# Delta stage of a hybrid DeltaNet and attention encoder: the first step of each group is stored and loaded ahead, GpSimd takes some elimination columns, the scaling moves

## The chip, the cores and the metric

The kernel runs on one core of a Trainium2 chip. The metric is the device time of the whole program in microseconds, the lower the better. Three runs of the kernel before took 4063.66, 4072.95 and 4077.66 us; the median is 4072.95 us.

## The reference, cut to what matters

The model has two layers over 2048 tokens of width 1024. In each layer one projection feeds two branches: a bidirectional gated DeltaNet with 4 heads of 128, and a grouped-query attention. Their gated outputs go through one output projection. The change touches the DeltaNet branch only, whose core is this recurrence, run once forward and once on the flipped sequence:

```python
lower = jnp.where(strict, jnp.einsum('bnhid,bnhjd->bnhij', k_beta, kc) * decay, 0.0)
a_mat = lower + jnp.eye(C, dtype=lower.dtype)
sol = lax.linalg.triangular_solve(a_mat, rhs, left_side=True, lower=True, unit_diagonal=True)
u, w = sol[..., :Dv], sol[..., Dv:]
def step(state, inp):
    v_new = u_i - jnp.einsum('bhcd,bhde->bhce', w_i, state)
    o_i = (jnp.einsum('bhcd,bhde->bhce', q_i * jnp.exp(g_i)[..., None], state)
           + jnp.einsum('bhij,bhje->bhie', a_i, v_new))
    state = state * jnp.exp(g_last)[..., None] + jnp.einsum('bhcd,bhce->bhde', k_dec, v_new)
```

So each chunk of tokens needs the inverse of a triangular matrix with ones on its diagonal, and the chunks of a direction follow each other through the state.

## The kernel before, in words

The program is a sequence of stages for each layer: input projection, tables, delta stage (`delta_net`), attention, output projection. The stages are separated by barriers. Inside a stage each engine works through its own list in the written order, and semaphores tie the lists together. All DMAs of the delta stage are issued by SyncE (SP), in the order in which its list is written; SP stands still at a wait, and everything later in its list stands with it.

The delta stage works on 16 chunks of 128 tokens (`NC = 16`), 4 heads, and two sides (forward and backward). It has two phases.

In the local phase TensorE forms the products k k^T and k q^T of every chunk, and VectorE multiplies them with the decays (`products`, L1438 and L1441) into `w` and `att`. SP stores the diagonal blocks of 32 x 32 of each `w` to DRAM (`w_blk`) and loads them back so that each of up to 128 partitions, a lane, holds one block. A block is inverted by elimination of 31 columns (`eliminate`); a column is a multiplication and a subtraction over all lanes. There are four groups of lanes (`GROUP_STEPS`): group 0 holds the blocks of scan steps 0 to 3, group 1 those of steps 4 to 7, and so on. Two sets of lane buffers are used in turn. Group 0 is eliminated on VectorE between the chunks (`LOCAL_COLS`), the others on GpSimd during the scan (`SCAN_COLS`: in scan step j, which group and how many columns). Afterwards `scale_lanes` (VectorE, L1467 and L1469) and `turn_lanes` (ScalarE, L1272) produce the scaled and the turned form, and SP stores both to DRAM (`store_lanes`, L1011 and L1015, four DMAs of 256 KB; the semaphores are `dt_stored` and `dd_stored`).

In the scan step j takes one chunk of each side. Its matrix inverse is put together from the 32 x 32 inverses, one step ahead: `load_dt(i)` and `load_dd(i)` (L1031, four DMAs of 32 KB each) bring the blocks of step i into `dt` and `dd`, which share the buffer `c_sq_acc`. TensorE multiplies `w` with `dt` (`off_diagonal`), VectorE masks it (`masked_blocks`, L1483), and three rounds of `substitute` on TensorE and `update` on VectorE (L1492, L1495) use `dd`. TensorE's order in step j is: `known`, `carried`, `off_diagonal(j+1)`, `solve(j)`, `turn_k(j+1)`, `substitute(j+1, 1)`, `output(j)`, `substitute(j+1, 2)`, `state_step(j)`, `substitute(j+1, 3)`. VectorE's order is: `remainder(j)` (L1476), `masked_blocks(j+1)`, `update(j+1, 1)`, `visit(j)` (L1505), `update(j+1, 2)`, `new_state(j)` (L1510), `update(j+1, 3)`, and in the steps of `SCALED` the scaling at the end. From step 8 on the output of a chunk is also joined, normalized and gated, and steps after 8 carry that work of the step before.

The four lane stores take 4 steps each as their outermost dimension (`i` in `i (h b) (s t)`). In SP's loop they stood first, in the steps of `STORED` (2, 6 and 9), that is one step after the scaling:

```python
for j in range(NC):
    if j in STORED: store_lanes(STORED[j])
    if j + 2 < NC: load_kq(j + 2)
    if j + 2 < NC: load_dt(j + 2)
    ...
    if j + 2 < NC: load_dd(j + 2)
```

Of the kernel before, what the change touches and what calls it, by code (L numbers as in the profile page):

```python
# [854 lines left out]
GROUP_STEPS = [(0, 4), (4, 8), (8, 12), (12, 16)]  # L855
GROUP_READY = [8, 16]
HALF_LANES = P // 2
CHUNK_LANES = DN_HEADS * N_BLK
# [2 lines left out]
FIRST_VISITS = NC // 2  # L861
COLS = BLK - 1
PARTS = 2 * COLS
LOCAL_COLS = {9: 1, 10: 5, 11: 5, 12: 5, 13: 5, 14: 5, 15: 5}
SCAN_COLS = {0: (1, 14), 1: (1, 17), 2: (2, 9), 3: (2, 10), 4: (2, 12), 5: (3, 9), 6: (3, 11), 7: (3, 11)}
SCALED = {1: 1, 5: 2, 8: 3}
STORED = {2: 1, 6: 2, 9: 3}
LANES_IN = {0: 2, 3: 3}

# [47 lines left out]
def delta_net(nc, a, c, l):  # L918
# [1 line left out]
    names = " ".join(f"{n}{side}" for n in per_side.split() for side in SIDES)  # L920
    names += (" kqv_loaded0 kqv_loaded1 kqv_loaded2 beta_loaded logs sums dts gram qk "
              "vt w att vv w_stored0 w_stored1 zeroed kq_loaded0 kq_loaded1 dt_loaded dd_loaded "
              "lane_loaded0 lane_loaded1 inv_set mat_set part turned scaled dt_stored dd_stored part_stored part_loaded z_loaded "
              "norm_loaded joined squared summed mean root inv_mean normed y_stored")
    with ExitStack() as stack, semaphores(nc, names) as s:
        b = Buffers(nc, stack, f"dn{l}")
# [30 lines left out]
        with nc.Block() as block:  # L957

            @block.sync
            def _(sp):  # L960
# [38 lines left out]
                                     a.b_rows[chunk_of(1, first + m), DN_HEADS:ITEMS].rearrange("h (b s) -> (h b) s", s=BLK)) \  # L999
                            .then_inc(s["beta_loaded"], 16)  # L1000

                def store_lanes(g):
                    first, last = GROUP_STEPS[g]
                    lower = slice(0, (last - first) * CHUNK_LANES)
                    upper = slice(HALF_LANES, HALF_LANES + (last - first) * CHUNK_LANES)
                    if g:
                        sp.wait_ge(s["dt_stored"], 32 * g)
                        sp.wait_ge(s["dd_stored"], 32 * g)
                    sp.wait_ge(s["scaled"], 2 * g + 2)
                    for side, src in enumerate((lanes.mat(g)[lower], lanes.mat(g)[upper])):  # L1010
                        sp.dma_start(a.d_blk[1, first:last, side].rearrange("i h b s t -> i (h b) (s t)"), src) \  # L1011
                            .then_inc(s["dt_stored"], 16)
                    sp.wait_ge(s["turned"], g + 1)
                    for side, src in enumerate((lanes.inv(g)[lower], lanes.raw(g)[upper])):
                        sp.dma_start(a.d_blk[0, first:last, side].rearrange("i h b s t -> i (h b) (s t)"), src) \  # L1015
                            .then_inc(s["dd_stored"], 16)

                def load_kq(i):
                    for side in SIDES:
# [3 lines left out]
                        sp.dma_start(kq[:, i % 2, side], a.proj[T_Q:T_K + DN_HEADS, :, at:at + P].rearrange("f p t -> p f t")) \  # L1023
                            .then_inc(s[f"kq_loaded{i % 2}"], 16)

                def load_blocks(tile, kind, i, loaded, stored):
                    group = sum(i >= last for _, last in GROUP_STEPS)
                    sp.wait_ge(stored, 32 * (group + 1))
                    for k in range(N_BLK):
                        at = slice(k * BLK, (k + 1) * BLK)  # L1030
                        sp.dma_start(tile[at].rearrange("p d h t -> p (d h) t")[:, :, at],  # L1031
                                     a.d_blk[kind, i, :, :, k].rearrange("d h s t -> s (d h) t")).then_inc(loaded, 16)

                def load_dt(i):
                    if i:
                        for side in SIDES:
                            sp.wait_ge(s[f"bt{side}"], i)
                    load_blocks(dt, 1, i, s["dt_loaded"], s["dt_stored"])

                def load_dd(i):  # L1040
                    if i:
                        for side in SIDES:
                            sp.wait_ge(s[f"y{side}"], 3 * i)
                    load_blocks(dd, 0, i, s["dd_loaded"], s["dd_stored"])

                def store_part(i):
                    for side in SIDES:
# [37 lines left out]
                        load_kq((n - 12) // 2)  # L1085
                load_lanes(1)
                sp.wait_ge(s["zeroed"], 2)
                store_lanes(0)
                load_dt(0)
                load_dd(0)  # L1090
                load_dt(1)
                load_dd(1)
                for j in range(NC):
                    if j in STORED:
                        store_lanes(STORED[j])
                    if j + 2 < NC:
                        load_kq(j + 2)
                    if j + 2 < NC:
                        load_dt(j + 2)
                    if j > FIRST_VISITS:  # L1100
                        store_y(j - 1)
                    if j in LANES_IN:
                        load_lanes(LANES_IN[j])
                    if j < FIRST_VISITS:
                        store_part(j)
                    else:
                        load_z(j)
                    if FIRST_VISITS <= j + 1 < NC:
                        load_part(j + 1)
                    if j + 2 < NC:  # L1110
                        load_dd(j + 2)
# [144 lines left out]
            def _(act):  # L1256
# [63 lines left out]
                for j in range(NC):  # L1320
                    for side in SIDES:
                        decayed_state(side, j)
                    if j > FIRST_VISITS:
                        root_mean(j - 1)
                    for side in SIDES:
                        carried_output(side, j)
                    for side in SIDES:
                        new_values(side, j)
                    if j + 1 < NC:
                        for side in SIDES:  # L1330
                            keys(side, j + 1)
                    if j in SCALED:
                        turn_lanes(SCALED[j])
                root_mean(NC - 1)

            @block.gpsimd
            def _(pool):
# [7 lines left out]

                def identity(g):
                    if g >= 2:
                        pool.wait_ge(s["dt_stored"], 32 * (g - 1))
                        pool.wait_ge(s["dd_stored"], 32 * (g - 1))
                    nc.gpsimd.memset(lanes.inv(g), 0.0).then_inc(s["inv_set"], 1)  # L1350
                    pool.wait_ge(s["inv_set"], 2 * g + 1)
                    nc.gpsimd.memset(lanes.diagonal(g), 1.0).then_inc(s["inv_set"], 1)
# [45 lines left out]
                for n in range(NC):  # L1398
                    token_logs(n)
                    if n in (3, 4):  # L1400
                        identity(n - 3)
                    if n == 5:
                        for tile in (dt, dd):
                            nc.gpsimd.memset(tile[:], 0.0).then_inc(s["zeroed"], 1)
                        for side in SIDES:
                            nc.gpsimd.memset(state[:, side], 0.0).then_inc(s[f"state{side}"], 1)
                pool.wait_ge(s["att"], NC)
                for side in SIDES:
                    masked_scores(side, 0)
                done = [0] * len(GROUP_STEPS)  # L1410
                for j in range(NC):
                    if j > FIRST_VISITS:
                        for side in SIDES:
# [20 lines left out]
            def _(dve):  # L1434
# [104 lines left out]
                for n in range(NC):  # L1539
                    products(n)  # L1540
                    if n == 9:
                        prepare_lanes(0)
                    if n in LOCAL_COLS:
                        eliminate(0, done, LOCAL_COLS[n])
                        done += LOCAL_COLS[n]
                scale_lanes(0)
                prepare_lanes(1)
                for side in SIDES:
                    masked_blocks(side, 0)
                for k in (1, 2, 3):  # L1550
# [2 lines left out]
                for j in range(NC):  # L1553
                    more = j + 1 < NC
                    if j > FIRST_VISITS:
                        for side in SIDES:
                            mean_squares(side, j - 1)
                    for side in SIDES:
                        remainder(side, j)
                    if j > FIRST_VISITS:  # L1560
                        inverse_root(j - 1)
                    if more:
                        for side in SIDES:
                            masked_blocks(side, j + 1)
                    if j > FIRST_VISITS:
                        for side in SIDES:
                            gate(side, j - 1)
                    if more:
                        for side in SIDES:
                            update(side, j + 1, 1)  # L1570
                    for side in SIDES:
                        visit(side, j)
                    if more:
                        for side in SIDES:
                            update(side, j + 1, 2)
                    for side in SIDES:
                        new_state(side, j)
                    if more:
                        for side in SIDES:
                            update(side, j + 1, 3)  # L1580
                    if j in SCALED:
                        scale_lanes(SCALED[j])
                for side in SIDES:
                    mean_squares(side, NC - 1)
                inverse_root(NC - 1)
# [694 lines left out]
```

## Time and profile before

| | us |
|---|---|
| median of 3 runs | 4072.95 |
| the profiled execution, whole | 4074.22 |
| its span | 4072.4 |
| TensorE (PE) busy | 3745.9 (92%) |
| VectorE (DVE) busy | 2774.2 (68%) |
| ScalarE (ACT) busy | 1877.4 (46%) |
| GpSimd (POOL) busy | 640.8 (16%) |
| delta stage of the first layer | about 680 to 1080 |
| delta stage of the second layer | about 2680 to 3085 |

Times in the rows count from the start of the span. A row of the order in time gives the start, the busy time, the engine, the line of the kernel, the operation, the tile written and the tiles read, shapes and the count; the square bracket at its end is the idle time of the engine just before it and what ended that. In the names `dn_sb_room` is the working buffer of the delta stage, `dn_sb_kq` the keys and queries of a step, and `c_sq_acc` holds `dt` and `dd`. PEclk is TensorE's granted clock as a share of full speed. The DMA share is the mean busy share of 16 DMA engines.

### The profile page before, as it was taken

What the parts mean: (1) busy time and instruction counts of PE and PEld (TensorE: products, weight loads), DVE (VectorE), ACT (ScalarE), POOL (GpSimd) and SP (SyncE); (2) the same over time, 40 slices, a digit from 0 to 9 for tenths busy, and PEclk for the clock granted to TensorE, in tenths of its full rate; (3) what the DMA queues carried; (4) which work ended last, traced back from release to release, by engine and by line L of the source; (5) the groups of instructions that cost most, each with busy time, mean ns of one, the idle gap of its engine ahead of it and who ended that gap; (6) DMA issues with size and microseconds to landing.
All of it is one profiled execution on the core that took longest, in us unless ns stands there. A gap on an engine that the chain in (4) does not pass through costs nothing. (4 is left out here: it accounts for less than half of the span.)

```text
span 4072.4 us, 55417 instructions
## 1 busy us (share of the span) xinstructions
PE 3745.9 (92%) x18982; PEld 2916.2 (72%) x18982; DVE 2774.2 (68%) x3394; ACT 1877.4 (46%) x2560; POOL 640.8 (16%) x637
## 2 busy tenths in 40 slices
PE   7999997699799999999899999976997999999895
PEld 5877785598667676667678777855895767777674
DVE  6674183666699999975266723836577999999743
ACT  4132212255377777772132222133554777777511
POOL 0022101396300000000001211035852000000000
PEclk9999998899899999999999999988998999999997
DMA  3111174546530000005321113654565100000335
GB/s 119 73 68 73 65 247 155 144 121 174 134 118 22 25 22 25 22 22 187 148 99 68 63 73 127 228 161 112 141 166 181 32 25 22 25 22 21 98 142 232
DMA packets 335332, 407.42 MB, mean 100 GB/s; under 512 B 105825, under 2 KB 254945, under 8 KB 314921
## 3 DMA queue, kind: packets, MB, share of 16 engines
q1 hardware_dynamic: 332152, 384.41, 29.6%
q10 hardware_dynamic: 3024, 20.97, 1.2%
q8 instruction: 94, 1.54, 0.2%
q14 instruction: 62, 0.50, 0.0%
HBM read 265.44 MB, written 139.66 MB: 99 GB/s over the span
## 5 line engine op out<-in xcount | busy, mean ns | idle before, releaser
L1829 DVE TENSOR_REDUCE att_sb_part<-att_banks 128x1 f32<-128x512 f32 x992 | 680.2, 686 | 101.5 <-PE att_banks L1714 87.4
L1816 ACT ACTIVATE att_sb_probs<-att_banks 128x1024 f32<-128x1024 f32 x512 | 525.1, 1025 | 312.7 <-PE att_banks L1742 312.5
L1847 DVE TENSOR_TENSOR att_sb_p_lo<-att_sb_probs,att_sb_p_hi 128x1024 fp32r<-128x1024 f32 x512 | 622.6, 1216 | 19.6 <-ACT att_sb_p_hi L1820 19.5
L1820 ACT ACTIVATE att_sb_p_hi<-att_sb_probs 128x1024 fp32r<-128x1024 f32 x512 | 544.1, 1063 | 16.2
L328 PE MATMUL proj_banks<-proj_sb_h_hi,proj_sb_w_hi 128*128 128x512 f32 x1600 | 500.6, 394 | 13.4 <-DVE proj_sb_pad L522 13.4
L328 PE MATMUL proj_banks<-proj_sb_h_lo,proj_sb_w_hi 128*128 128x512 f32 x1600 | 498.7, 393 | 0.0
L328 PE MATMUL proj_banks<-proj_sb_h_hi,proj_sb_w_low 128*128 128x512 f32 x1600 | 497.8, 392 | 0.0
L1742 PE MATMUL att_banks<-att_sb_q,att_sb_k 68*128 68x512 f32 x1024 | 408.7, 399 | 0.0
L1741 PE MATMUL att_banks<-att_sb_q,att_sb_k 128*128 128x512 f32 x1024 | 406.3, 397 | 1.9 <-DVE att_sb_q L1841 1.9
L1759 PE MATMUL att_banks<-att_sb_p_hi,att_sb_v_hi 128*65 128x512 f32 x1024 | 403.1, 394 | 1.4 <-DVE att_sb_p_lo L1847 1.4
L388 POOL TENSOR_TENSOR c_low_squares<-c_sq_acc,proj_sb_high_squares 128x2048 fp32r<-128x2048 f32 x28 | 141.1, 5038 | 1671.3 <-ACT c_sq_acc L449 1671.3
L1759 PE MATMUL att_banks<-att_sb_p_lo,att_sb_v_hi 128*65 128x512 f32 x1024 | 402.8, 393 | 0.0
L1714 PE MATMUL att_banks<-att_sb_k,att_sb_q 128*128 128x512 f32 x992 | 398.9, 403 | 3.0 <-DVE att_sb_part L1829 2.8
L1759 PE MATMUL att_banks<-att_sb_p_hi,att_sb_v_lo 128*65 128x512 f32 x1024 | 400.8, 391 | 0.0
L328 PEld LDWEIGHTS proj_banks<-proj_sb_h_hi,proj_sb_w_hi 128*128 128x128 f32 x1600 | 301.5, 189 | 88.4 <-issue 14.7
L328 PEld LDWEIGHTS proj_banks<-proj_sb_h_lo,proj_sb_w_hi 128*128 128x128 f32 x1600 | 301.0, 188 | 75.5
L328 PEld LDWEIGHTS proj_banks<-proj_sb_h_hi,proj_sb_w_low 128*128 128x128 f32 x1600 | 301.0, 188 | 72.2
L1119 PE MATMUL dn_banks<-dn_sb_room 128*128 128x128 f32 x2048 | 263.6, 283 | 37.1 <-DMA dn_sb_room<-proj 20.2
L1119 PEld LDWEIGHTS dn_banks<-dn_sb_room 128*128 128x128 f32 x2048 | 249.3, 197 | 58.3 <-DMA dn_sb_room<-proj 25.9
L595 DVE SCALAR_TENSOR_TENSOR proj_sb_out<-proj_sb_pad,proj_sb_taps,proj_sb_out 128x2048 f32<-128x2048 f32 x96 | 276.7, 2882 | 3.4
L522 DVE TENSOR_TENSOR proj_sb_out<-proj_banks,proj_sb_scale 128x1024 f32<-128x1024 f32 x56 | 68.5, 1223 | 272.5 <-PE proj_banks L328 272.5
L1714 PEld LDWEIGHTS att_banks<-att_sb_k,att_sb_q 128*128 128x128 f32 x992 | 189.5, 191 | 79.0 <-DVE att_sb_part L1829 7.0
(229 smaller groups left out, 5337.3 us busy)
## 6 DMA issues: line engine op xcount, KB each, us to landing
proj<-proj_sb_out SPq DMA_DIRECT2D x40, 1024.0 KB, 3.8
dn_sb_kq<-proj SPq DMA_DIRECT2D x64, 512.0 KB, 5.0
proj_sb_w_raw<-in_w_in SPq DMA_DIRECT2D x52, 536.0 KB, 3.6
dn_sb_room<-proj SPq DMA_DIRECT2D x32, 768.0 KB, 4.9
att_sb_q<-att_q SPq DMA_DIRECT2D x64, 256.0 KB, 2.6
x_res<-ahead_delta SPq DMA_DIRECT2D x16, 1024.0 KB, 4.1
proj_sb_pad<-proj SPq DMA_DIRECT2D x24, 512.0 KB, 4.4
proj<-proj_sb_out ACTq DMA_DIRECT2D x12, 1024.0 KB, 4.4
```

Of the source, the lines that this page charges most:

```text
L328: mm = nc.tensor.matmul(ps[:, 2 * half + n, :], w[:, u, k, :], h[:, k, at:at + QB], start=(k == 0 and w is w_hi and h is h_hi), stop=(k == ...
L388: nc.gpsimd.tensor_tensor(low, raw, high[:].bitcast(F32), ALU.subtract).then_inc(s["squares_split"], 1)
L595: nc.vector.scalar_tensor_tensor(out=out[:, u, :], in0=src, scalar=taps[:, u, j:j + 1], in1=out[:, u, :], op0=ALU.mult, op1=ALU.add).then_ ...
L1119: mm = nc.tensor.matmul(out[:, h, :], left[:, h, :], right[:, h, :], start=True, stop=True)
L1714: nc.tensor.matmul(ps[:, 4 + u % 2, :], q1[:, slot, tile * P:(tile + 1) * P], k1[:, slot % 2, keys * QB:(keys + 1) * QB], start=True, stop ...
L1741: nc.tensor.matmul(out, k1[:, slot % 2, keys], q1[:, slot, :], start=True, stop=False)
L1742: mm = nc.tensor.matmul(out, k2[:, slot % 2, keys], q2[:, slot, :], start=False, stop=True)
L1759: mm = nc.tensor.matmul(ps[0:DH + 1, 6 + kv, :], part_v[:, kv, tile, 0:DH + 1], part_p[:, at, m, :], start=opens, stop=(tile == NC - 1 and ...
L1816: nc.scalar.activation(probs[:, pair % 2], ps[:, 2 * (pair % 2):2 * (pair % 2) + 2, :], ACT.Exp, scale=SCALE).then_inc(s["exp_done"], 1)
L1820: nc.scalar.activation(p_hi[:, pair % SLOTS], probs[:, pair % 2], ACT.Copy).then_inc(s["hi_done"], 1)
L1829: nc.vector.tensor_reduce(part[:, w // NQ, w % NQ:w % NQ + 1], ps[:, 4 + w % 2, :], AX.X, ALU.max) \
L1847: nc.vector.tensor_tensor(p_lo[:, pair % SLOTS], probs[:, pair % 2], p_hi[:, pair % SLOTS].bitcast(F32), ALU.subtract).then_inc(s["lo_done ...
```

## The change

Four things change, all in `delta_net`.

1. Group 0's elimination: in the chunks 11 to 15 of the local phase GpSimd takes one column (`BESIDE_COLS`) while VectorE does the products, and VectorE takes 4 instead of 5. The results are chained through the semaphore `part` as before.
2. Group 1: VectorE does its first 6 columns (`AHEAD_COLS`) right after it prepared the lanes, before the scan. GpSimd's share in the steps 0 and 1 falls from 14 and 17 to 12 and 13.
3. `store_lanes` is cut in two: `store_first` stores the first step of a group (four DMAs of 64 KB), `store_rest` the other three steps (four DMAs of 192 KB), with semaphores of their own. `load_dt` and `load_dd` wait for the one or the other, by the step they load. Before the scan the order on SP is now first, `load_dt(0)`, `load_dd(0)`, rest, `load_dt(1)`, `load_dd(1)`. In SP's loop the stores moved from the beginning of steps 2, 6, 9 to the middle of steps 2, 5, 8.
4. `scale_lanes` stands in the middle of a step, between `update(j+1, 1)` and `visit(j)`, in steps 2, 5, 8 (before: at the end of steps 1, 5, 8). `turn_lanes` on ScalarE stands ahead of `keys`.

```diff
-LOCAL_COLS = {9: 1, 10: 5, 11: 5, 12: 5, 13: 5, 14: 5, 15: 5}
-SCAN_COLS = {0: (1, 14), 1: (1, 17), 2: (2, 9), 3: (2, 10), 4: (2, 12), 5: (3, 9), 6: (3, 11), 7: (3, 11)}
-SCALED = {1: 1, 5: 2, 8: 3}
-STORED = {2: 1, 6: 2, 9: 3}
+LOCAL_COLS = {9: 1, 10: 5, 11: 4, 12: 4, 13: 4, 14: 4, 15: 4}
+BESIDE_COLS = {11: 1, 12: 1, 13: 1, 14: 1, 15: 1}
+AHEAD_COLS = 6
+SCAN_COLS = {0: (1, 12), 1: (1, 13), 2: (2, 9), 3: (2, 10), 4: (2, 12), 5: (3, 9), 6: (3, 11), 7: (3, 11)}
+SCALED = {2: 1, 5: 2, 8: 3}
...
+                def store_steps(g, lo, hi, dt_sem, dd_sem):
+                    lower = slice((lo - GROUP_STEPS[g][0]) * CHUNK_LANES, (hi - GROUP_STEPS[g][0]) * CHUNK_LANES)
+                    upper = slice(HALF_LANES + lower.start, HALF_LANES + lower.stop)
+                    for side, src in enumerate((lanes.mat(g)[lower], lanes.mat(g)[upper])):
+                        sp.dma_start(a.d_blk[1, lo:hi, side].rearrange("i h b s t -> i (h b) (s t)"), src).then_inc(dt_sem, 16)
+                    sp.wait_ge(s["turned"], g + 1)
+                    for side, src in enumerate((lanes.inv(g)[lower], lanes.raw(g)[upper])):
+                        sp.dma_start(a.d_blk[0, lo:hi, side].rearrange("i h b s t -> i (h b) (s t)"), src).then_inc(dd_sem, 16)
+                def store_first(g):
+                    if g:
+                        sp.wait_ge(s["dt_first"], 32 * g)
+                        sp.wait_ge(s["dd_first"], 32 * g)
+                    sp.wait_ge(s["scaled"], 2 * g + 2)
+                    store_steps(g, GROUP_STEPS[g][0], GROUP_STEPS[g][0] + 1, s["dt_first"], s["dd_first"])
...
-                    sp.wait_ge(stored, 32 * (group + 1))
+                    sp.wait_ge(first if i == GROUP_STEPS[group][0] else rest, 32 * (group + 1))
...
-                store_lanes(0)
+                store_first(0)
                 load_dt(0)
                 load_dd(0)
+                store_rest(0)
                 load_dt(1)
                 load_dd(1)
                 for j in range(NC):
-                    if j in STORED:
-                        store_lanes(STORED[j])
                     if j + 2 < NC:
                         load_kq(j + 2)
+                    soon = j in SCALED and GROUP_STEPS[SCALED[j]][0] == j + 2
+                    if soon:
+                        store_first(SCALED[j])
                     if j + 2 < NC:
                         load_dt(j + 2)
+                    if j in SCALED:
+                        if not soon:
+                            store_first(SCALED[j])
+                        store_rest(SCALED[j])
...
+                col = 0
+                for n in LOCAL_COLS:
+                    if n in BESIDE_COLS:
+                        eliminate(0, col, BESIDE_COLS[n])
+                        col += BESIDE_COLS[n]
+                    col += LOCAL_COLS[n]
                 pool.wait_ge(s["att"], NC)
...
                 scale_lanes(0)
                 prepare_lanes(1)
+                eliminate(1, 0, AHEAD_COLS)
...
+                    if j in SCALED:
+                        scale_lanes(SCALED[j])
                     for side in SIDES:
                         visit(side, j)
```

GpSimd's `identity` waits for all four store semaphores of the group that used the buffers before.

## Rows read from the trace of the kernel before

**Rows 1.** The waits of the delta stage, first layer; columns: who, for whom, us in total, times, longest.

```profile
PE dn_banks L1119 <- DMA c_sq_acc<-d_blk: 38.0, 5, 29.4
```

**Rows 2.** TensorE in order of time, start of the scan and a plain step, first layer.

```profile
792.48 3.75 PE L1119 MATMUL dn_banks<-c_sq_acc,dn_sb_w 128*128 128x128 f32 x16 [29.44 <-DMA c_sq_acc<-d_blk]
...
801.49 3.84 PE L1119 MATMUL dn_banks<-dn_sb_state,dn_sb_kq 128*128 128x128 f32 x32
...
816.67 3.84 PE L1119 MATMUL dn_banks<-dn_sb_state,dn_sb_kq 128*128 128x128 f32 x32
...
820.35 1.95 PE L1119 MATMUL dn_banks<-c_sq_acc,dn_sb_w 128*128 128x128 f32 x16
...
824.79 1.95 PE L1119 MATMUL dn_banks<-c_sq_acc,dn_sb_room 128*128 128x128 f32 x16
...
831.86 3.84 PE L1119 MATMUL dn_banks<-dn_sb_state,dn_sb_kq 128*128 128x128 f32 x32
```

**Rows 3.** TensorE in order of time, later step starts and one wait, first layer.

```profile
873.00 3.84 PE L1119 MATMUL dn_banks<-dn_sb_state,dn_sb_kq 128*128 128x128 f32 x32
...
903.38 3.84 PE L1119 MATMUL dn_banks<-dn_sb_state,dn_sb_kq 128*128 128x128 f32 x32
...
918.81 3.84 PE L1119 MATMUL dn_banks<-dn_sb_state,dn_sb_kq 128*128 128x128 f32 x32
...
926.63 3.78 PE L1119 MATMUL dn_banks<-c_sq_acc,dn_sb_w 128*128 128x128 f32 x16 [3.97 <-DMA c_sq_acc<-d_blk]
...
940.59 3.84 PE L1119 MATMUL dn_banks<-dn_sb_state,dn_sb_kq 128*128 128x128 f32 x32
...
993.57 3.84 PE L1119 MATMUL dn_banks<-dn_sb_state,dn_sb_kq 128*128 128x128 f32 x32
...
1009.63 3.84 PE L1119 MATMUL dn_banks<-dn_sb_state,dn_sb_kq 128*128 128x128 f32 x32
```

**Rows 4.** TensorE in order of time, start and step 11 of the scan, second layer.

```profile
2792.79 3.75 PE L1119 MATMUL dn_banks<-c_sq_acc,dn_sb_w 128*128 128x128 f32 x16 [29.04 <-DMA c_sq_acc<-d_blk]
...
2997.77 3.84 PE L1119 MATMUL dn_banks<-dn_sb_state,dn_sb_kq 128*128 128x128 f32 x32
```

**Rows 5.** VectorE in order of time: products, a column, the scaling of groups 0 and 1.

```profile
757.04 0.68 DVE L1438 TENSOR_TENSOR dn_sb_w<-dn_banks,dn_sb_room 128x512 f32<-128x512 f32 x1
...
758.24 0.41 DVE L1453 TENSOR_TENSOR dn_sb_lane_tmp<-dn_sb_lane_mat,dn_sb_lane_inv 128x255 f32<-128x255 f32 x1
...
773.47 1.87 DVE L1467 TENSOR_TENSOR dn_sb_lane_mat<-dn_sb_lane_inv,dn_sb_lane_beta 64x1024 f32<-64x1024 f32 x1
...
835.67 2.90 DVE L1467 TENSOR_TENSOR dn_sb_lane_mat<-dn_sb_lane_inv,dn_sb_lane_beta 64x1024 f32<-64x1024 f32 x1 [3.03 <-POOL dn_sb_lane_inv L1364]
```

**Rows 6.** SP's DMA issues in order of time, first layer.

```profile
776.67 1.20 SPq L1011 DMA_DIRECT2D d_blk<-dn_sb_lane_mat  x2
...
780.32 1.23 SPq L1015 DMA_DIRECT2D d_blk<-dn_sb_lane_raw  x1
...
786.66 17.08 SPq L1031 DMA_DIRECT2D c_sq_acc<-d_blk  x16
...
832.71 1.80 SPq L1031 DMA_DIRECT2D c_sq_acc<-d_blk  x4
```

**Rows 7.** Windows: stretch, length, busy us of the engines, PEclk, DMA share, GB/s.

```profile
784.00:786.00 2.00, 0.00 (x0) 0.00 (x0) 0.00 (x0) 0.00 (x0) 1.69 (x5) 0.50 0.25 104
```

**Rows 8.** DMA issues by tile: count, KB each, median us to landing; 840 to 857, then 680 to 1060.

```profile
dn_sb_kq<-proj SPq DMA_DIRECT2D x2, 512.0 KB, 8.9
...
dn_sb_lane_raw<-w_blk SPq DMA_DIRECT2D x16, 64.0 KB, 2.9
```

**Rows 9.** GpSimd in order of time, first instruction of a column.

```profile
818.00 0.66 POOL L1362 TENSOR_TENSOR dn_sb_lane_tmp<-dn_sb_lane_mat,dn_sb_lane_inv 128x255 f32<-128x255 f32 x1
```

**Rows 10.** VectorE in order of time, inside plain step 1: visit and new state.

```profile
827.67 0.69 DVE L1505 TENSOR_TENSOR dn_sb_room<-dn_banks,dn_sb_room 128x512 f32<-128x512 f32 x1 [0.20 <-PE dn_banks L1119]
...
830.55 0.69 DVE L1510 TENSOR_TENSOR dn_sb_state<-dn_sb_room,dn_banks 128x512 f32<-128x512 f32 x1 [0.51 <-PE dn_banks L1119]
```

More of the change, by code:

```diff
@@ L922, in delta_net @@
               "vt w att vv w_stored0 w_stored1 zeroed kq_loaded0 kq_loaded1 dt_loaded dd_loaded "
-              "lane_loaded0 lane_loaded1 inv_set mat_set part turned scaled dt_stored dd_stored part_stored part_loaded z_loaded "
+              "lane_loaded0 lane_loaded1 inv_set mat_set part turned scaled dt_first dd_first dt_stored dd_stored part_stored part_loaded z_loaded "
               "norm_loaded joined squared summed mean root inv_mean normed y_stored")
@@ L1000, in load_beta, with store_rest @@
                             .then_inc(s["beta_loaded"], 16)
[L1002 to L1005, printed above, removed]
+                def store_steps(g, lo, hi, dt_sem, dd_sem):
[12 more added lines that the diff above has]
+                    store_steps(g, GROUP_STEPS[g][0], GROUP_STEPS[g][0] + 1, s["dt_first"], s["dd_first"])
+                def store_rest(g):
                     if g:
@@ L1008, in store_lanes @@
                         sp.wait_ge(s["dd_stored"], 32 * g)
[L1009 to L1016, printed above, removed]
+                    store_steps(g, GROUP_STEPS[g][0] + 1, GROUP_STEPS[g][1], s["dt_stored"], s["dd_stored"])
                 def load_kq(i):
@@ L1024, in load_kq, with load_blocks @@
                             .then_inc(s[f"kq_loaded{i % 2}"], 16)
-                def load_blocks(tile, kind, i, loaded, stored):
+                def load_blocks(tile, kind, i, loaded, first, rest):
                     group = sum(i >= last for _, last in GROUP_STEPS)
-                    sp.wait_ge(stored, 32 * (group + 1))
+                    sp.wait_ge(first if i == GROUP_STEPS[group][0] else rest, 32 * (group + 1))
                     for k in range(N_BLK):
@@ L1037, in load_dt @@
                             sp.wait_ge(s[f"bt{side}"], i)
-                    load_blocks(dt, 1, i, s["dt_loaded"], s["dt_stored"])
+                    load_blocks(dt, 1, i, s["dt_loaded"], s["dt_first"], s["dt_stored"])
                 def load_dd(i):
@@ L1043, in load_dd @@
                             sp.wait_ge(s[f"y{side}"], 3 * i)
-                    load_blocks(dd, 0, i, s["dd_loaded"], s["dd_stored"])
+                    load_blocks(dd, 0, i, s["dd_loaded"], s["dd_first"], s["dd_stored"])
                 def store_part(i):
@@ L1328, in _ @@
                         new_values(side, j)
+                    if j in SCALED:
+                        turn_lanes(SCALED[j])
                     if j + 1 < NC:
@@ L1331, in _ @@
                             keys(side, j + 1)
-                    if j in SCALED:
-                        turn_lanes(SCALED[j])
                 root_mean(NC - 1)
@@ L1347, in identity @@
                     if g >= 2:
-                        pool.wait_ge(s["dt_stored"], 32 * (g - 1))
-                        pool.wait_ge(s["dd_stored"], 32 * (g - 1))
+                        for stored in ("dt_first", "dd_first", "dt_stored", "dd_stored"):
+                            pool.wait_ge(s[stored], 32 * (g - 1))
                     nc.gpsimd.memset(lanes.inv(g), 0.0).then_inc(s["inv_set"], 1)
@@ L1409, in _ @@
                     masked_scores(side, 0)
-                done = [0] * len(GROUP_STEPS)
+                done = [0, AHEAD_COLS, 0, 0]
                 for j in range(NC):
@@ L1542, in _ @@
                         prepare_lanes(0)
+                    if n in BESIDE_COLS:
+                        done += BESIDE_COLS[n]
                     if n in LOCAL_COLS:
@@ L1570, in _ @@
                             update(side, j + 1, 1)
+                    if j in SCALED:
+                        scale_lanes(SCALED[j])
                     for side in SIDES:
@@ L1580, in _ @@
                             update(side, j + 1, 3)
-                    if j in SCALED:
-                        scale_lanes(SCALED[j])
                 for side in SIDES:
```

## The prediction, made before the kernel ran

> **What bounds the kernel now.** I began with the page: TensorE is busy 92% of the span, so only its idle stretches can be won, and the change touches only the delta stage, which runs once in each of the two layers. The waits of that stage come next. There the matmuls stand 38.0 us on transfers into the block tiles (`c_sq_acc<-d_blk`, which are `dt` and `dd`), 29.4 us of it in one piece [rows 1]. The order in time shows the places. TensorE is idle 29.44 us before the scan (792.48), and its first matmuls then run slowly: step 0 begins 9.01 us later, at 801.49. A plain step takes 816.67 to 831.86 = 15.19 us; in it the off-diagonal product, which needs `dt` of the next step, starts 3.7 us in, and the first substitution, which needs `dd` of the next step, 8.1 us in [rows 2]. A late step with output normalization takes 1009.63 - 993.57 = 16.06 us [rows 3].
>
> Everything above that is a stretch. From step 0 (801.49) to step 11 (993.57) are 192.08 us; nine plain steps and two late ones would be 9 x 15.19 + 2 x 16.06 = 168.83, so layer 1 loses 23.25 us [rows 2, 3]. In the second layer, from the first matmul (2792.79) to step 11 (2997.77) are 204.98 us; less 9.01 and 168.83 this leaves 27.14 us [rows 4]. Layer 1 loses them so: steps 2 and 3, 873.00 - 831.86 - 30.38 = 10.76 us; steps 6 to 10, 993.57 - 903.38 - 3 x 15.19 - 2 x 16.06 = 12.5 us [rows 2, 3]. The first comes from the scaling of group 1: VectorE waits 3.03 us for GpSimd's columns, then scales at 2.90 us an instruction where 1.87 us was the time alone [rows 5]. Step 7 shows a late `dt`: TensorE waits 3.97 us, the next 16 matmuls take 3.78 us instead of 1.95, and the step is 940.59 - 918.81 - 15.19 = 6.6 us longer [rows 2, 3]. So a wait of about 4 us costs 2.6 us more through the lower clock.
>
> **How the group stores leave.** This decides the sum. The four stores of a group (1 MB) are issued from 776.67 to 781.55. The load of `dt` may start when the first two have landed, at 786.66, 10.0 us after their issue, and TensorE gets `dt` at 792.48, 15.8 us after the first issue [rows 2, 6]. In that time the DMA share is 0.25 at 104 GB/s: 4 engines of 16, 26 GB/s each [rows 7]. The stores' outermost dimension is the 4 steps of a group. A transfer that uses all engines waits behind them: the `kq` load next in SP's order takes 8.9 us to land, though it moves data at once on the idle engines [rows 8].
>
> **1. Five columns of group 0 on GpSimd.** On VectorE the two products of a chunk take 758.24 - 757.04 = 1.20 us; a column there is two instructions of 0.41 us with gaps, about 0.9 us for the longest and 0.65 for short ones. GpSimd needs two of 0.66 us and gaps, 1.5 us for the longest [rows 5, 9]. The products read PSUM, and in the rows they keep their 0.68 us. So the GpSimd column is hidden but for 0.3 us: 0.6 to 0.7 us won five times, 3.2 us. Bounds: 0 to 4.3. It counts in full, since VectorE has no gap between the chunks. The first store goes out at 773.45 instead of 776.67.
>
> **2. First step stored apart (group 0).** Each of these stores has 16 rows of 4 KB. The nearest row is the lane load of the same shape: 64 KB land in 2.9 us [rows 8]. SP issues four small DMAs in 1.8 us (832.71), which I take for the four stores and for each set of four loads [rows 6]. `dt` stores out at 773.45 and 773.9, landed 776.8; `load_dt(0)` 776.8 to 778.6, landed 781.0. TensorE starts 11.5 us earlier (11 to 13), step 0 at 790.0.
> Then `load_dd(0)` to 780.4, and the rest of the group (768 KB) goes out. Its outermost dimension is 3 steps, so by the same pattern 3 engines with 256 KB each, exactly the bytes per engine of before. `load_dt(1)` stands behind it and lands 15.8 us later, at 796.2; step 0 wants it at 790.0 + 3.7 = 793.7. Wait 2.5 us and clock: 5.1 us (0 to 6) given back.
>
> **3. Six columns of group 1 on VectorE, its scaling in the middle of step 2.** The six columns (about 3.5 us) lie in VectorE's idle time before the first block product: nothing. GpSimd has fewer columns left (25 instead of 31) and no longer makes VectorE wait. The scaling now stands before `visit`, 10.8 us into the step. Alone it takes 3.2 us (from 773.47 to the first store at 776.67 [rows 5, 6]); beside GpSimd's columns, by 2.90 against 1.87, up to 5. I take 4.2, the middle, since at the 2.90 GpSimd worked on masked scores, longer instructions than columns. Before the new state VectorE has 0.20 and 0.51 us of idle time [rows 10], and 0.6 us lie between the state and the next product. So a step with scaling grows by 4.2 - 1.3 = 2.9 us (1.9 in step 8, where GpSimd has no columns) and is 18.1 us long. Bounds: 1.9 to 3.7. ACT's turn falls where it waits for the state product: nothing.
>
> **4. What SP now holds back.** In loop j SP issues `load_kq`, `load_dt`, then the stores, and only then `store_part` and `load_dd(j+2)`. Before, the stores came one loop later, when the scaling was already done. Now SP waits at them for the scaling of the same step; `dd` of step j+2 stands behind them in SP's order and then behind the rest's 256 KB on three engines. Substitution 1 of step j+1 needs it.
> Group 1 (j = 2, times from the start of step 2): scaled 15.0; first stores landed 18.35; `load_dt(4)` to 20.15, landed 22.6, wanted at 18.1 + 3.7 = 21.8: 0.8 late. The rest goes out at 20.15; a load behind it lands 15.8 later, and the 512 KB of `store_part` at 16 x 26 GB/s add 1.3: `dd(4)` at 37.25. From the substitution to the next step are 7.1 us, plus 2.6 for the clock: step 4 at 46.95. Plain would be 30.38: 16.6 us lost, where 10.76 was.
> Group 2 (j = 5): scaled 15.0, rest out 16.8, `dd(7)` at 16.8 + 15.8 + 1.3 = 33.9, wanted at 18.1 + 8.1 = 26.2. Step 7 at 33.9 + 9.7 = 43.6: 13.2 lost.
> Group 3 (j = 8): scaled 14.0, rest out 15.8, z and part loads add 2.5: `dd(10)` at 34.1. Step 10 at 43.8 against 31.25: 12.55 lost.
>
> **The sum.** Lost in the scan after the change: 5.1 + 16.6 + 13.2 + 12.55 = 47.45 us. Layer 1: 47.45 - 23.25 - 11.5 = +12.7. Layer 2: 47.45 - 27.14 - 11.5 = +8.8. Together +21.5 on the profiled execution's 4074.2 us, which stands 1.3 us above the median of the three runs: 4094 us.
>
> **The rivals.**
> A, the forecast: the rest stores keep 3 engines busy and hold `dd`. 4094 (4080 to 4110), chance 0.57.
> B, faster: a store of 3 steps is spread over all 16 engines (it has 48 rows). It then drains within its issue time of 4.9 us; step 0 doesn't wait, `dd(4)` lands 30.4 after step 2's start (9.7 lost with the clock), `dd(7)` and `dd(10)` are 0.7 and 0.8 late (3.6 and 2.7 lost with the scaling). 16.0 - 23.25 - 11.5 and 16.0 - 27.14 - 11.5: -41.4, 4032 us. Against it: the 4-step store has 64 rows and used 4 engines [rows 7]. It decides from about 10 engines on, where 768 KB drain in 3 us. Chance 0.20.
> C, the rest drains at 26 GB/s per engine from its first byte: 256 / 26 = 9.8 us, and a load behind lands 11.8 after, not 15.8. Step 0 has no wait, the three others lose 4 less: 17.1 less per layer, 4060 us; halfway it is 4077. 
>
> The Trainium skill, "DMA: Bandwidth & Descriptors", section "Why a DMA increments its semaphore by 16 and not by 1", has a rule on this: the number of engines is the largest, up to 16, that divides the slowest dimension not of size 1 on both sides. The share of 0.25 agrees for the whole group. For the new shapes it gives 3 and 16; no row of before shows them. By it B and D would fall and A would stand.
>
> **Chances.** No change is what lies within 0.3% (12 us), about what this kernel's runs can tell. Faster: B, and 0.05 of C: 0.25. The same: 0.09 of C and 0.11 of A: 0.20. Slower: the rest of A, D, 0.02 of C: 0.55. The range 4030 to 4112 takes in B's time and leaves out D and the tails; the likeliest case alone would be 4080 to 4110.
>
> **What would show it.** Right: the first block product near 781 us, after less than 20 us of idle time instead of 29.4; then TensorE waits of 8 to 11 us on `c_sq_acc<-d_blk` at the first substitution of steps 3, 6 and 9, in both layers; a DMA share near 0.19 for 10 us after each rest; the scaling at 4 us or less and followed by `visit`; no wait of VectorE for GpSimd before it. Wrong: waits on `dd` under 3 us, or a share near 1 after the rest stores (B); a first matmul later than 785 us (D).

## The result, and the profile after

The changed kernel takes 4125.1 us (median of 4 runs, 4119.3 to 4125.7) against 4074.9 us before (4 runs, 4063.7 to 4077.7): a ratio of 1.0129, 95% interval 1.0115 to 1.0144. It is slower by 50 us, where 4094 was forecast and 4112 was the upper end. The profiled execution took 4125.4 us with a span of 4123.6, 51.2 us longer than before.

The waits of the first delta stage in the changed kernel, to be read beside [rows 1] of before:

```profile
PE dn_banks L1134 <- DMA c_sq_acc<-d_blk: 46.9, 5, 17.2
```

TensorE in order of time there (start, us, operation, idle time before and its releaser), against [rows 2, 3]: the first block product, the starts of the steps (the rows that read `dn_sb_state`: steps 0 to 5, 7, 8, 10 and 11) and the waits on `dt` (rows with `dn_sb_w`) and `dd` (rows with `dn_sb_room`) between them.

```profile
776.54 3.75 PE L1134 MATMUL dn_banks<-c_sq_acc,dn_sb_w 128*128 128x128 f32 x16 [17.23 <-DMA c_sq_acc<-d_blk]
785.15 3.84 PE L1134 MATMUL dn_banks<-dn_sb_state,dn_sb_kq 128*128 128x128 f32 x32
792.86 3.78 PE L1134 MATMUL dn_banks<-c_sq_acc,dn_sb_w 128*128 128x128 f32 x16 [3.88 <-DMA c_sq_acc<-d_blk]
807.28 3.84 PE L1134 MATMUL dn_banks<-dn_sb_state,dn_sb_kq 128*128 128x128 f32 x32
822.46 3.84 PE L1134 MATMUL dn_banks<-dn_sb_state,dn_sb_kq 128*128 128x128 f32 x32
839.63 5.47 PE L1134 MATMUL dn_banks<-dn_sb_state,dn_sb_kq 128*128 128x128 f32 x32 [0.28 <-DVE dn_sb_state L1531]
858.83 3.79 PE L1134 MATMUL dn_banks<-c_sq_acc,dn_sb_room 128*128 128x128 f32 x16 [9.28 <-DMA c_sq_acc<-d_blk]
868.26 3.84 PE L1134 MATMUL dn_banks<-dn_sb_state,dn_sb_kq 128*128 128x128 f32 x32
...
883.45 3.84 PE L1134 MATMUL dn_banks<-dn_sb_state,dn_sb_kq 128*128 128x128 f32 x32
...
916.48 3.78 PE L1134 MATMUL dn_banks<-c_sq_acc,dn_sb_room 128*128 128x128 f32 x16 [7.80 <-DMA c_sq_acc<-d_blk]
926.09 3.84 PE L1134 MATMUL dn_banks<-dn_sb_state,dn_sb_kq 128*128 128x128 f32 x32
941.28 3.84 PE L1134 MATMUL dn_banks<-dn_sb_state,dn_sb_kq 128*128 128x128 f32 x32
...
975.90 3.79 PE L1134 MATMUL dn_banks<-c_sq_acc,dn_sb_room 128*128 128x128 f32 x16 [8.70 <-DMA c_sq_acc<-d_blk]
984.85 3.84 PE L1134 MATMUL dn_banks<-dn_sb_state,dn_sb_kq 128*128 128x128 f32 x32
1000.91 3.84 PE L1134 MATMUL dn_banks<-dn_sb_state,dn_sb_kq 128*128 128x128 f32 x32
```

The reader sees the forecast picture: TensorE starts after 17 us of idle time instead of 29, and then waits 7.8 to 9.3 us for `dd` at the first substitution of steps 3, 6 and 9. Step 11 begins at 1000.91, 7.3 us later than before [rows 3]. The second layer's first block product and step 11, against [rows 4]:

```profile
2790.18 3.75 PE L1134 MATMUL dn_banks<-c_sq_acc,dn_sb_w 128*128 128x128 f32 x16 [17.25 <-DMA c_sq_acc<-d_blk]
...
3014.80 3.84 PE L1134 MATMUL dn_banks<-dn_sb_state,dn_sb_kq 128*128 128x128 f32 x32
```

There the changed kernel is 3014.80 - 2997.77 = 17.0 us behind, with nearly all of both delta stages done. At the end of the span it is 51.2 us behind, so 34.2 us are lost later, where the diff changes nothing. The waits of the second attention stage (3130 to 3830 us) in the changed kernel:

```profile
ACT att_sb_probs L1840 <- PE att_banks L1766: 159.6, 223, 3.7
DVE att_sb_part L1853 <- PE att_banks L1738: 45.4, 121, 1.4
DVE att_sb_part L1853 <- issue: 27.1, 5, 5.7
...
PEld att_banks L1738 <- DVE att_sb_part L1853: 22.6, 7, 4.3
ACT att_sb_probs L1840 <- DVE att_sb_p_lo L1871: 22.3, 5, 4.7
PE att_banks L1738 <- DVE att_sb_part L1853: 18.9, 7, 3.9
```

The same view of the kernel before (3113 to 3813 us):

```profile
ACT att_sb_probs L1816 <- PE att_banks L1742: 155.5, 236, 2.6
DVE att_sb_part L1829 <- PE att_banks L1714: 40.7, 125, 1.4
...
PEld att_banks L1714 <- DVE att_sb_part L1829: 1.9, 2, 1.1
```

"issue" says that VectorE waited for nothing that the profile shows, 27.1 us in five pieces; the kernel before has no such row in this window. (Both kernels have one other wait with "issue", of 6.1 to 7.1 us, ahead of the loop, at the start of each attention stage.) Two of them in VectorE's order of time, 95.7 us apart, which is one pass of its loop over the attention blocks; a loop of six passes has five back branches:

```profile
3315.91 0.69 DVE L1853 TENSOR_REDUCE att_sb_part<-att_banks 128x1 f32<-128x512 f32 x1 [5.31 <-issue]
...
3411.62 0.69 DVE L1853 TENSOR_REDUCE att_sb_part<-att_banks 128x1 f32<-128x512 f32 x1 [5.71 <-issue]
```

The DMA view of that stage (queue, packets, MB, share) counts the transfers of instructions: 32 in the changed kernel,

```profile
q14 instruction: 32, 0.26, 0.1%
```

and 8 before:

```profile
q14 instruction: 8, 0.07, 0.0%
```

So the suspicion is that VectorE fetches its loop anew at each back branch, the jump from the end of the loop to its start. In the compiled program of the kernel before, VectorE's second attention loop begins at instruction 2856 and its back branch is instruction 3115, 259 further on; the change adds 4 VectorE instructions per layer, so it begins at 2864. The same loop in the first layer, moved by 4 places, shows no such wait in either kernel.

### The profile page after: what moved, and what is told of

Same layout as the page of the kernel before. It is cut to its first block and busy times, and to the rows that moved or that the text cites. A ratio compares the mean times of both kernels' runs of the same rounds, so it can differ in the third digit from the quotient of the medians.

```text
span 4123.6 us, 55463 instructions
## 1 busy us (share of the span) xinstructions
PE 3764.3 (91%) x18982; PEld 2929.8 (71%) x18982; DVE 2767.2 (67%) x3398; ACT 1877.4 (46%) x2560; POOL 638.7 (15%) x633
```

## The experiments

Each one was timed beside the kernel before on its own chip; a ratio is to those runs. Medians of different chips differ by a few us for the same kernel (4070.2 to 4074.9 for the kernel before), so gains between two chips are given relative to their own runs of before. The theories are P (placement of VectorE's loop, against D, something that the delta stage leaves behind) and Q with O (SP is held up by stores on three engines, and by its order, against S, the scaling).

**b_pad8.** The kernel before, its loop moved to where the change put it.

```diff
                 done = 0
+                for n in range(8 if l == 1 else 0):
+                    nc.vector.memset(pad[:, n:n + 1], 0.0)
                 for n in range(NC):
                     products(n)
```

> The kernel before, with eight one-element memsets on VectorE at the start of the second layer's delta stage (nothing reads them; about 0.06 us each, under 0.5 us in all). They put VectorE's second attention loop 8 instructions later in its program, at the very place where the changed kernel has it (instruction 2864 instead of 2856). Theory P (placement: the changed kernel's 34 us in the second attention stage are VectorE fetching its loop anew at each of 5 back branches): the kernel before now shows the same five stalls of L1853 with no releaser, 27 us in all, about 30 instruction packets on q14 in that stage, and 4074 + 34 = about 4108 us. Rival D (the 34 us come from what the delta stage leaves behind: another order of transfers, another state of the queues or of the clock): 4074 us, no such stalls.

4106.1 us, ratio 1.0082 (1.0065 to 1.0099). Eight instructions that do nothing cost 33 to 36 us, and the stall is there, 28.1 us where the changed kernel has 27.1:

```profile
DVE att_sb_part L1832 <- issue: 28.1, 5, 5.8
```

with 31 instruction packets. No part of the change is in this kernel, so D is out and the place alone brings the stall. What it costs shows in the length of the second attention stage, from the memset that opens it to the first `out_sb_w_lo` behind it: 740.9 us in the kernel before, 774.7 in the changed one and 778.2 here. Over all traces it is 774.7 to 778.2 us in the four kernels whose loop begins at 2864 (the changed one, b_pad8, a_spread, a_dd_first) and 740.8 to 744.9 in the nine others, whatever their delta stage does: P is shown.

**a_pad8** and **a_pad64.** The same lines with 8 and 64 in the changed kernel.

> The changed kernel with the same eight memsets: the second attention loop stands at instruction 2872 of VectorE's program instead of 2864. Theory P: if only a loop that begins at the very end of a stretch of instructions is fetched anew, the stalls go: 4125 - 34 = about 4091 us, with the delta stage's losses unchanged. If the bad places reach further than 8 instructions, it stays at 4125. Rival D: 4125 us.

> The changed kernel with 64 such memsets (about 4 us of VectorE at the start of the second layer's delta stage, where it waits for its first load anyway, so at most some us): the loop stands at instruction 2928. Theory P: no stalls, 4091 us (up to 4095 with the memsets). Rival D: 4125 us or a few more.

4095.3 us, ratio 1.0055 (1.0038 to 1.0072), and 4090.2 us, ratio 1.0049 (1.0032 to 1.0066). The row of this loop with "issue" is gone from both, and the second attention stage of a_pad8, 743.4 us long, has:

```profile
q14 instruction: 7, 0.06, 0.0%
```

So the change proper costs 20 to 25 us; 21.5 was forecast.

**b_pad4** and **b_pad12.** The edges, one run each.

> How wide the bad place is: the kernel before with four memsets, loop at instruction 2860. At 2856 it ran without stalls, at 2864 with five. If the bad stretch is only the few places where a loop of 260 instructions reaches into a third block of 256: no stalls, about 4074 us; if it begins between 2857 and 2860: 4108 us.

> The other edge: twelve memsets, loop at instruction 2868 (2872 ran without stalls). If the bad stretch is as narrow as the loop's excess over 256 instructions (some four places): no stalls, about 4074 us; else 4108 us.

4067.8 and 4069.0 us, each with 7 instruction packets in the stage and no such wait; with one run each it is the traces that decide. If the bad places lie together, they lie between 2861 and 2867. The Trainium skill, "Runtime: NRT & Kernel Launch", section "Instruction fetch mechanics", says that most engines hold two blocks of 256 instructions and that a branch to a target outside them waits for a fetch. A loop of 259 or 260 instructions needs a third block only from two or three of 256 places, which agrees with at most seven bad ones here. That the blocks are the cause is argued from the Trainium skill, and where the blocks begin is not known here; the runs show the stall, its place and its price.

**a_spread.** The changed kernel with one store per step.

```diff
-    sp.dma_start(a.d_blk[1, lo:hi, side].rearrange("i h b s t -> i (h b) (s t)"), src).then_inc(dt_sem, 16)
+    for i in range(lo, hi):
+        at = slice((i - lo) * CHUNK_LANES, (i - lo + 1) * CHUNK_LANES)
+        sp.dma_start(a.d_blk[1, i, side].rearrange("h b s t -> (h b) (s t)"), src[at]).then_inc(dt_sem, 16)
```

The stores of `d_blk[0]` go the same way, and the waits for the rest count 96 instead of 32 per group.

> The changed kernel, only that each store of lanes over several steps is one transfer per step (16 partitions of 4 KB each) instead of one over three steps: 12 transfers instead of 4 for a group's rest, whose packets then lie on all 16 DMA engines instead of 3. Order on SP and all else as in the changed kernel, VectorE's program too, so the 34 us in attention stay. Theory Q (the waits of 9.3, 7.8 and 8.7 us on dd per layer are SP held up by the rest stores on three engines): SP issues the four dd loads in about 2 us instead of 6.65 and they land in 3, so 6 to 7 us go at each of six places, and some of step 0's 3.8: 4125 - 40 = about 4085 us. Rival S (the waits come from scaling in the middle of the step, which makes y late, or from SP's order alone): within 5 us of 4125.

4071.1 us, ratio 1.0002 (0.9992 to 1.0011). The changed kernel is 50.2 us above its own runs of before, this one 0.9: 49 us gained (52 by the ratios), where 40 was expected. A window beside the rest store of group 1 (stretch, length, busy us of PE, PEld, DVE, ACT and POOL, PEclk, DMA share, GB/s) in the changed kernel,

```profile
844.00:846.00 2.00, 2.00 (x20) 2.00 (x20) 0.48 (x2) 1.76 (x7) 1.76 (x4) 1.00 0.17 43
```

and with spread stores:

```profile
838.00:840.00 2.00, 2.00 (x20) 2.00 (x20) 0.62 (x1) 1.76 (x7) 1.84 (x4) 1.00 0.84 152
```

A share of 0.17 is about 3 engines of 16 (3/16 is 0.19, and the window before, 842 to 844, has 0.19); spread it is 0.84. SP then issues the four loads of `dd` in 2.00 us instead of 6.65; the changed kernel's SP rows (start, us, operation, count):

```profile
841.18 1.45 SPq L1009 DMA_DIRECT2D d_blk<-dn_sb_lane_mat  x2
842.67 2.10 SPq L1012 DMA_DIRECT2D d_blk<-dn_sb_lane_inv  x1
844.81 1.09 SPq L1012 DMA_DIRECT2D d_blk<-dn_sb_lane_raw  x1
845.95 1.02 SPq L1058 DMA_DIRECT2D dn_part<-dn_sb_room  x2
847.09 6.65 SPq L1040 DMA_DIRECT2D c_sq_acc<-d_blk  x4
```

and with spread stores:

```profile
836.16 2.71 SPq L1011 DMA_DIRECT2D d_blk<-dn_sb_lane_mat  x6
838.92 1.34 SPq L1016 DMA_DIRECT2D d_blk<-dn_sb_lane_inv  x3
840.31 1.35 SPq L1016 DMA_DIRECT2D d_blk<-dn_sb_lane_raw  x3
841.70 0.90 SPq L1065 DMA_DIRECT2D dn_part<-dn_sb_room  x2
842.70 2.00 SPq L1047 DMA_DIRECT2D c_sq_acc<-d_blk  x4
```

TensorE's wait for `dd(4)` falls from 9.28 to 3.43 us:

```profile
846.32 3.78 PE L1141 MATMUL dn_banks<-c_sq_acc,dn_sb_room 128*128 128x128 f32 x16 [3.43 <-DMA c_sq_acc<-d_blk]
```

The scaling stood where it was, so S is out for these waits. Six waits on `dd` of 0.2 to 4.2 us are left, 15 us in both layers together; they belong to SP's order, as the next experiment and a_both_pad8 show.

**a_dd_first.** The changed kernel, only SP's order.

```diff
                         if not soon:
                             store_first(SCALED[j])
-                        store_rest(SCALED[j])
...
                     if j + 2 < NC:
                         load_dd(j + 2)
+                    if j in SCALED:
+                        store_rest(SCALED[j])
```

> The changed kernel with one call moved on SP: store_rest of a group stands at the end of step j, behind load_dd(j + 2), instead of behind load_dt(j + 2); the rest stores keep their three engines, VectorE's program is the same, so the 34 us in attention stay. Theory O (SP's order is the cause): dd comes in time and the six waits of 8 to 11 us on it, 53 us in all, go; but the rest store now starts some 15 us later and drains over three engines, so load_dt of the group's second step, which waits for it, comes late and gives about half back: about 4100 us. Theory E (the three engines are the cause, whichever order): the late dt costs as much as the late dd did, 4120 to 4130 us.

4088.7 us, ratio 1.0031 (1.0018 to 1.0043). It stands 13.8 us above its own runs of before, so against the changed kernel the order alone is worth 36 us (40 by the ratios). The six waits on `dd`, 53.4 us in all, are gone, and `dt` of the group's second step is late instead, by 1.9 to 5.2 us each time, 20.3 us in all:

```profile
864.49 3.61 PE L1135 MATMUL dn_banks<-c_sq_acc,dn_sb_w 128*128 128x128 f32 x16 [5.05 <-DMA c_sq_acc<-d_blk]
```

O holds, with less given back than expected (4100); E, by which the order would not matter, is out. The gains of spread stores and of the order are not to be added: each takes away part of the same waits.

**a_both_pad8.** Spread stores, this order, and the loop moved.

> All three together: the changed kernel with one store per step (all 16 engines), store_rest behind load_dd, and the eight memsets that move VectorE's loop. The one with the spread stores alone ran 4071 us; less 34 us for the loop; less its six remaining waits on dd (3.4, 0.2, 4.2, 2.5, 1.6 and 3.3 us, 15 in all): about 4022 us, if the late rest store does not make dt late. If it does: 4037 us or more.

4014.1 us (4005.4 to 4022.1), ratio 0.9864 (0.9842 to 0.9887): 61 us below the kernel before by the medians, and the fastest of all; 4022 was expected. After its start TensorE waits for no transfer into the block tiles in the first scan; the group's only row is the one before the first block product:

```profile
PE dn_banks L1143 <- DMA c_sq_acc<-d_blk: 16.1, 1, 16.1
```

**b_spread.** The kernel before with its four-step stores split in the same way.

> The kernel before, only that each store of a group's lanes is one transfer per step (16 transfers of 16 partitions instead of 4 over four steps), on all 16 engines instead of four. VectorE's program is unchanged. Of the 23 and 27 us that its two scans lose against plain steps, the waits behind the stores go in part; the wait for the first block product (29 us, stores and loads in a row) gets some us shorter too: about 4045 us. Rival: before's loads wait for scaling and for the order on SP and not for the draining: 4070 us.

4048.7 us, ratio 0.9936 (0.9914 to 0.9957), near the expected 4045: 26 us gained. The change on top of spread stores is then worth another 35 us (4014.1), if SP's order and the loop's place are put right.

**b_cols_pad16.** The kernel before with the columns of the change alone.

```diff
-LOCAL_COLS = {9: 1, 10: 5, 11: 5, 12: 5, 13: 5, 14: 5, 15: 5}
-SCAN_COLS = {0: (1, 14), 1: (1, 17), 2: (2, 9), ...
+LOCAL_COLS = {9: 1, 10: 5, 11: 4, 12: 4, 13: 4, 14: 4, 15: 4}
+BESIDE_COLS = {11: 1, 12: 1, 13: 1, 14: 1, 15: 1}
+AHEAD_COLS = 6
+SCAN_COLS = {0: (1, 12), 1: (1, 13), 2: (2, 9), ...
```

> The kernel before with only the columns changed as in the change: one of each of group 0's last five blocks of columns on GpSimd beside the products, six columns of group 1 ahead of the scan on VectorE; stores, loads and scaling as before. Sixteen unused memsets keep VectorE's second attention loop (at instruction 2878) off the place where it stalled. Step 1 of the prediction: 3.2 us a layer, 4074 - 6 = about 4067 us. Rival: VectorE waits for GpSimd's column as long as its own took: 4074 us.

4060.8 us, ratio 0.9975 (0.9964 to 0.9985): 14 us by the medians, not 6. Group 0 is faster by about what was expected: from the products of chunk 10 to the scaling VectorE needs 30.09 us (738.76 to 768.85), where it needed 32.88 (740.59 to 773.47). The rest comes from the scan, which the expectation had left out: with 25 columns instead of 31 GpSimd is done sooner, and the first scaling (at 827.71) no longer waits for it, where it waited 3.03 us [rows 5]. From the first block product to step 11 it takes 197.93 us instead of 201.09, and in the second layer 199.39 instead of 204.98.

**a_both_whole.** The fastest kernel with group 0 stored whole before its first loads.

```diff
                 store_first(0)
+                store_rest(0)
                 load_dt(0)
                 load_dd(0)
-                store_rest(0)
```

> The fastest one so far (spread stores, store_rest behind load_dd, loop moved), only that in group 0 store_rest stands ahead of load_dt(0) and load_dd(0): the first step is no longer ahead of the rest. It tells what the early first step is worth once the stores leave on all engines. Twelve more stores stand before load_dt(0) on SP, about 0.4 us each. If the first block product comes as late as with the kernel before and spread stores (24 us of idle time instead of 16): 8 us in each layer, 4014 + 16 = about 4030 us. Rival: with spread stores the order does not matter: 4014 to 4018.

4026.0 us, ratio 0.9882 (0.9864 to 0.9899), where 4030 was expected. Against a_both_pad8 that is 12 us more by the medians but 7 by the ratios, whose intervals overlap, so the times alone do not settle it; the traces do. The wait before the first block product is 22.15 us instead of 16.10, in the second layer 21.91 instead of 16.07:

```profile
784.52 3.73 PE L1143 MATMUL dn_banks<-c_sq_acc,dn_sb_w 128*128 128x128 f32 x16 [22.15 <-DMA c_sq_acc<-d_blk]
```

So the early first step is worth 6 us a layer once the stores leave on all engines; with whole groups on four engines before and the rest on three after, it was worth 10.

## Why the prediction was right and wrong

**1. Five columns on GpSimd, 3.2 us.** Right: 2.8 us, borne out by b_cols_pad16. From the products of chunk 10 to the scaling the changed kernel takes 767.70 - 737.61 = 30.09 us, before it was 32.88. VectorE waits 0.18 to 0.32 us for GpSimd's column.

**2. First step stored apart, 11.5 us with the columns.** Right, a little short: from the scaling to the first block product are 776.54 - 767.70 = 8.84 us, before 19.01 [rows 2, 5], so 10.2 us, and 13.0 with the columns. The forecast moment 781.0 came at 776.54, but 3.0 us of this were there when the products of chunk 10 began (737.61 against 740.59), ahead of the first column moved to GpSimd, and are not the change's. The `dt` wait in step 0 was 3.9 us, not 2.5, and the step lost 807.28 - 785.15 - 15.19 = 6.9 us, not 5.1. The 15.8 us that a load waits behind the stores came out as forecast: the rest goes out at 777.04 and TensorE gets `dt` of step 1 at 792.86.

```profile
777.04 1.61 SPq L1009 DMA_DIRECT2D d_blk<-dn_sb_lane_mat  x2
```

**3. Columns ahead and scaling in the middle.** Right in kind, too dear in size. The scaling beside GpSimd takes 3.6 us where 4.2 was taken:

```profile
833.18 2.18 DVE L1488 TENSOR_TENSOR dn_sb_lane_mat<-dn_sb_lane_inv,dn_sb_lane_beta 64x1024 f32<-64x1024 f32 x1
835.40 1.37 DVE L1490 TENSOR_TENSOR dn_sb_lane_mat<-dn_sb_lane_inv,dn_sb_lane_beta 64x1024 f32<-64x1024 f32 x1
836.80 1.29 DVE L1526 TENSOR_TENSOR dn_sb_room<-dn_banks,dn_sb_room 128x512 f32<-128x512 f32 x2
```

Step 2 took 839.63 - 822.46 = 17.2 us, 2.0 more than a plain step, not 2.9; the two other scaling steps 1.6 to 1.8. At the scaling VectorE no longer waits for GpSimd.

**4. What SP holds back.** Right in mechanism and size: the six waits on `dd` are 7.8 to 10.9 us, where 8 to 11 was named as the sign. Lost in steps 2 and 3: 868.26 - 822.46 - 30.38 = 15.4 us (forecast 16.6); steps 5 and 6: 926.09 - 883.45 - 30.38 = 12.3 (13.2); steps 8 and 9: 984.85 - 941.28 - 31.25 = 12.3 (12.55). With step 0 that is 46.9 us in the first scan, against 47.45. That the total is off by only half a microsecond is luck: the terms are off by +1.8, -1.2, -0.9 and -0.2. The experiments bear the cause out from both sides: the engines (a_spread, 49 us) and the order (a_dd_first, 36 us).

**The sum of the delta stages.** +21.5 was forecast, +17.0 stands at step 11 of the second layer, and 20 to 25 us by the runs with the loop out of the bad place. So the central figure of 4094 was about right for the change proper. Rivals B, C and D did not occur: the share beside the rest stores was 0.17 to 0.19 and not near 1 (B), the load behind the rest landed after 15.8 us and not 11.8 (C), and the first block product came at 776.54, not after 785 (D).

**The step that failed** is the first sentence of the reading: "the change touches only the delta stage". It does in the source, not in the program. The sum had no term for what follows, where the same instructions stood 8 places later; it put that stage at nothing, and 34 us were lost there (stage length 774.7 us instead of 740.9). With the 17.0 of the delta stages these are the 51.2 us. Nothing in the rows of before shows this price: 8 instruction packets and no row with "issue" in the loop. What could have been seen is the exposure: behind the edited code stands a VectorE loop whose back branch is 259 instructions on. The Trainium skill, "Runtime: NRT & Kernel Launch", section "Instruction fetch mechanics", warns of branches out of the two blocks that an engine holds. A rival of this kind, with 5 back branches and an unknown price each, was missing, and so the range ended 13 us short.

## What to carry to other kernels

After a change, compare the traces at a landmark behind each stage, the unchanged ones too: here 17 us of the 51 were at the edit and 34 in a stage that the diff doesn't touch. Where an engine runs a loop, an edit ahead of it moves it: look for waits with "issue" once per pass and for more packets on the instruction queue, and settle it by padding the old kernel by as many instructions. Here a store whose outermost dimension was 4 steps kept the DMA share at 0.25 and one of 3 steps at 0.17 to 0.19, while stores of one step reached 0.84, and the few-engine stores held the issuing queue behind them. Splitting them by step gave 26 us to the old kernel and about 50 to the new one, and moving them behind the loads with a near due time gave 36.

## What the runs showed of the hardware

A back branch of VectorE's loop cost 5.2 to 5.8 us of its time from one placement (the loop beginning at 2864, in four kernels) and nothing that shows from six others (beginning at 2856, 2860, 2868, 2872, 2878 and 2928); with what waits for VectorE it was 34.2 / 5 = 6.8 us each. The changed kernel moved 24 more instruction packets in that stage than the kernel before, about 5 for each of these branches. The transfers of instructions during such a stall, in the DMA view of 3309 to 3317 us:

```profile
q14 instruction: 4, 0.03, 1.7%
```

Four packets of 8 KB took part in a stall of 5.31 us while the DMA share was 0.07 (3310.0 to 3315.5), so it is no matter of bandwidth. SP's issue of four block loads, 1.80 us in the kernel before [rows 6], took 6.65 us behind stores on three engines, 0.78 to 2.45 us for one issue where the median in that kernel is 0.45: the issuing itself slows down, and all that stands behind it in SP's order is late.
